# Modulation products: VectorE multiplies and adds up its units, TensorE only sums over the partitions, and its bank joins the ring

## The reference, cut to what matters

```python
mod = jax.nn.silu(c) @ mod_w[l] + mod_b[l]            # 1024 -> 3072
mod_k = jax.nn.silu(c_ctx) @ mod_w[l] + mod_b[l]      # the same matrix, a second vector
shift, scale, gate = jnp.split(mod[:, None, :], 3, axis=-1)
```

## Time and profile before

| | |
|---|---|
| Time, median of 3 runs | 3220.55 us (3218.56 to 3220.67) |
| The profiled execution | 3219.65 us, of which its span is 3217.9 us |
| TensorE busy | 3129.8 us, 97% of the span |
| VectorE busy | 2400.6 us, 75% |
| ScalarE busy | 1240.1 us, 39% |
| Chain that ended last | TensorE 87%, VectorE 8%, ScalarE 4% |
| Mean granted TensorE clock | 0.993 |

### The profile page before, as it was taken

How to read it: one execution, slowest core, us unless ns; L and a number is a source line. 1 busy time by engine, 2 the same in 40 slices (tenths; PEclk the granted TensorE clock), 3 DMA queues, 4 the chain that set the end, 5 groups by cost and what they waited for, 6 DMA issues and landing times.

```text
span 3217.9 us, 37930 instructions
## 1 busy us (share of the span) xinstructions
PE 3129.8 (97%) x14840; PEld 2545.9 (79%) x14840; DVE 2400.6 (75%) x4144; ACT 1240.1 (39%) x1933; POOL 2.2 (0%) x9
## 2 busy tenths in 40 slices
PE   8999999999999999988999999999999999999998
PEld 7878888877988877777878888888777687788887
DVE  6777677768869588878588767667688789789736
ACT  4333233335242455655243223223255533423414
POOL 0000000000000000000000000000000000000000
PEclk9999999999999999999999999999999999999999
DMA  3222212213433450002311111111211222122242
GB/s 128 72 79 79 72 59 73 66 59 125 123 88 126 142 191 8 7 27 90 133 53 46 59 46 53 59 46 53 66 53 52 107 74 70 40 73 93 82 170 73
DMA packets 89249, 250.68 MB, mean 78 GB/s; under 512 B 8560, under 2 KB 24304, under 8 KB 87536
## 3 DMA queue, kind: packets, MB, share of 16 engines
q1 hardware_dynamic: 89072, 248.25, 22.9%
HBM read 204.18 MB, written 44.04 MB: 77 GB/s over the span
## 4 chain that ended last, share of the span: by engine, by line
PE 87%; DVE 8%; ACT 4%; issue 1%; DMA 0%; DVEq 0%; SPq 0%; ACTq 0%
PE PS L543 85%; PE PS L548 2%; DVE WS L2167 1%; DVE X L2175 1%; DVE TMP L2167 1%; DVE X L2167 1%; ACT PT L1294 1%; DVE XS L2175 1%; ACT TMP L1772 1%; DVE COLB L2975 1%; ACT WS L1294 0%; ACT XS L1294 0%; DVE HELD L2224 0%; DVE XSf L2167 0%; DVE PT L2167 0%
## 5 line engine op out<-in xcount | busy, mean ns | idle before, releaser
L543 PE MATMUL PS<-XS,WS 128*128 128x512 f32 (+1 forms) x6480 | 1516.9, 391 | 18.1 <-DVE XS L2167 9.0
L543 PEld LDWEIGHTS PS<-XS,WS 128*128 128x128 f32 x6480 | 1210.3, 188 | 293.5 <-issue 28.8
L543 PE MATMUL PS<-HS,WS 128*128 128x512 f32 x2208 | 515.2, 393 | 13.5 <-DVE HS L2167 10.4
L543 PEld LDWEIGHTS PS<-HS,WS 128*128 128x128 f32 x2208 | 416.9, 189 | 105.3 <-DVE HS L2167 11.2
L1294 ACT ACTIVATE WS<-RAW 128x512 fp32r<-128x512 f32 (+1 forms) x390 | 305.1, 788 | 448.6 <-PE PS L543 393.2
L2167 DVE TENSOR_TENSOR WS<-RAW,WS 128x512 fp32r<-128x512 f32 (+1 forms) x390 | 344.5, 892 | 158.8 <-ACT WS L1294 157.9
L2167 DVE TENSOR_TENSOR X<-PS,X 128x512 f32<-128x512 f32 x272 | 184.4, 689 | 116.1 <-PE PS L543 116.0
L2167 DVE TENSOR_TENSOR TMP<-TMP,PS 128x512 f32<-128x512 f32 x304 | 203.7, 683 | 65.5 <-PE PS L543 59.3
L543 PE MATMUL PS<-T,WS 128*128 128x512 f32 x960 | 230.6, 389 | 0.0
L543 PEld LDWEIGHTS PS<-T,WS 128*128 128x128 f32 x960 | 180.2, 188 | 37.4
L1294 ACT ACTIVATE TMP<-PS 128x512 f32<-128x512 f32 x144 | 85.1, 595 | 306.0 <-PE PS L543 302.3
(11 more groups left out here) (334 smaller groups left out, 3643.4 us busy)
## 6 DMA issues: line engine op xcount, KB each, us to landing
RAW<-in_W SPq DMA_DIRECT2D x258, 512.0 KB, 3.4
RAWX<-in_W SPq DMA_DIRECT2D x35, 512.0 KB, 3.3
DC<-TMP SPq DMA_DIRECT2D x32, 256.0 KB, 2.1
X<-in_xT SPq DMA_DIRECT2D x8, 512.0 KB, 9.4
DX<-X SPq DMA_DIRECT2D x2, 2048.0 KB, 8.5
DCZ<-CA SPq DMA_DIRECT2D x8, 512.0 KB, 4.1
DGA<-TMP SPq DMA_DIRECT2D x16, 256.0 KB, 2.1
DGB<-TMP SPq DMA_DIRECT2D x16, 256.0 KB, 3.2
```

Of the source, the lines that this page charges most:

```text
L543: done = d.matmul(out, l, r, start=first, stop=last)
```

## The change

VectorE now reads a modulation unit raw. For each of its two blocks of 512 columns and each of the two vectors it multiplies by the vector's value of the partition and adds to `HELD`. Nothing is split, no place of `WS` is taken, and TensorE no longer multiplies the units. After four units TensorE sums `HELD` over the partitions by eight matmuls against one column of ones, each with a 128x128 block of `HELD` as fp32 weights. The doubled units lie in blocks 3, 6, 9 and 12 (before: 3, 5, 7 and 9), the turn stands behind m3 of the block that ends a group, and bank 7 is in the ring from the start. The raw slot of a modulation unit comes free when VectorE has worked it, and forms whose raw slot follows such a unit are not written before it is released. The four instructions of `sums` move from the m2 form to the m6 form in both networks.

```diff
-            for _ in range(2 if n in (3, 5, 7, 9) else 1):
+            for _ in range(2 if n in (3, 6, 9, 12) else 1):
                 out.append(("mod", mods))
                 mods += 1
+            turn = ("turn", mods // 4 - 1) if mods // 4 > turned else None
+            turned = mods // 4
         out += [("m1", n + 1) if n < 21 else ("m2", n), ("m4", n), ("m3", n)]
+        if with_mod and turn:
+            out.append(turn)
...
-        f.raws = [ends[earlier[n]] for n in f.loads if n in earlier and forms[ends[earlier[n]]].kind == "raw"]
+        f.raws = [ends[earlier[n]] for n in f.loads if n in earlier and forms[ends[earlier[n]]].kind in ("raw", "vec")]
...
-            sum_at[min(u, pieces[1])] = f.loads
+            sum_at[u] = f.loads
...
-    banks, tmps, misc = Ring(7), Ring(NTMP), Ring(2)
+    banks, tmps, misc = Ring(8), Ring(NTMP), Ring(2)
...
-            e.wait_ge(ac("mod", m), dma("const")("cols"), *banks.free(use))
-            trs([(bank(*use)[:, 4 * j:4 * j + 4], HELD[0:4, m % 2, 128 * j:128 * j + 128], ident[0:4, 0:4])
-                 for j in range(4)]).then_inc(*mm.inc(*use))
...
-            mms([(PS[0:4, 7, :], CVS[:, 2 * q + k, :], blk(us[k], 0, 512)[r], q + k + r == 0, q + k + r == 5)
-                 for k in range(2) for r in range(2)]).then_inc(*mm.inc("mod", n))
...
+            e.wait_ge(ve("mv", 4 * m + 3), ve("ones"), *banks.free(use))
+            for j in range(4):
+                for v in range(2):
+                    done = d.matmul(bank(*use)[:, 2 * j + v:2 * j + v + 1], HELD[:, v, 128 * j:128 * j + 128], ones[:, 0:1],
+                                    start=True, stop=True)
+            done.then_inc(*mm.inc(*use))
...
+        def mod_unit(n):
+            m, q = divmod(n, 4)
+            u = w.take()
+            e.wait_ge(*loaded(u), ac("cv"))
+            for k in range(2):
+                for v in range(2):
+                    x, c = HELD[:, v, :], cvec[:, 2 * q + k, v:v + 1]
+                    if q + k == 0:
+                        d.tensor_scalar(x, raw(u, 512 * k, 512), c, None, ALU.mult).then_inc(*ve.inc("ms", n, k, v))
+                    else:
+                        e.wait_ge(ve("ms", n, 0, v) if k else ve("ms", n - 1, 1, v))
+                        stt(x, raw(u, 512 * k, 512), c, x, ALU.mult, ALU.add).then_inc(*ve.inc("ms", n, k, v))
+            ve.same("mv", n)
+            ve.same("vec", u)
+            release(u)
...
-                if m == 1 and with_mod:
-                    mod_turn(5)
...
-                    e.wait_ge(mm("unit", u) if forms[u].kind == "raw" else w_lo(u))
+                    e.wait_ge(mm("unit", u) if forms[u].kind == "raw" else ve("vec", u) if forms[u].kind == "vec" else w_lo(u))
...
-            for a in (down(columns_of(n)) if what == "down" else [mod[n]]):
+            for a in down(columns_of(n)) if what == "down" else ():
                 k = load(a)
                 forms += [("cols", "turning", (k,), 0), ("cols", "turning", (k,), 1)]
+            if what == "mod":
+                forms.append(("vec", "turning", (load(mod[n]),), 0))
```

More of the change, by code:

```diff
@@ L34, in product_steps @@
 def product_steps(with_mod):
-    out, mods = [], 0
+    out, mods, turned = [], 0, 0
     for n in range(2, 22):
@@ L155, in lay_out @@
         forms.append(f)
-        if kind == "raw":
+        if kind in ("raw", "vec"):
             continue
@@ L228, in next_half @@
             self.halved += 1
-            if f.kind not in ("raw", "hold"):
+            if f.kind not in ("raw", "vec", "hold"):
                 return self.halved - 1
@@ L693, in ffn @@
                 elif what == "mod":
-                    mod_unit(n)
+                    release(w.take())
+                elif what == "turn":
+                    mod_turn(n)
                 else:
@@ L1268, in tensor @@
         ffn("ln1", "x", True)
-        banks.resize(8)
-        banks.ends[7] = ((ac, "mod", 5),)
         latents()
@@ L1396, in turned @@
                     act(hi(k), lo(k), ACT.Copy).then_inc(*ac.inc(name, what, k))
-            def mod_unit(n):
-                m, q = divmod(n, 4)
-                us = [w.take(), w.take()]
-                if q == 3:
-                    e.wait_ge(mm("mod", n))
-                    if m > 1:
-                        e.wait_ge(mm("mt", m - 2))
-                    act(HELD[0:4, m % 2, :], PS[0:4, 7, :], ACT.Copy).then_inc(*ac.inc("mod", m))
-                release(*us)
             us = {fi: (w.take(), w.take()) for fi in (0, 1)}
@@ L1428, in ffn @@
             for what, n in product_steps(with_mod):
+                if what == "turn":
+                    continue
                 if what == "mod":
-                    mod_unit(n)
+                    release(w.take())
                     continue
@@ L2274, in norm @@
                     yield
+        def mod_unit(n):
[13 more added lines that the diff above has]
+            release(u)
         def mod_turn(m):
             e.wait_ge(mm("mt", m), dma("const")("cols"))
-            part = bank("mt", m)[:, 0:16].rearrange("p (a r v) -> p a r v", a=4, r=2)
             out = MOD[:, 4 * m:4 * m + 4, :]
-            tt(out, part[:, :, 0], col("mod_b", 4 * m, 4).unsqueeze(2).to_broadcast([128, 4, 2]), ALU.add).then_inc(*ve.inc("mt0", m))
-            e.wait_ge(ve("mt0", m))
-            tt(out, out, part[:, :, 1], ALU.add).then_inc(*ve.inc("mt", m))
+            tt(out, bank("mt", m)[:, 0:8].rearrange("p (a v) -> p a v", v=2),
+               col("mod_b", 4 * m, 4).unsqueeze(2).to_broadcast([128, 4, 2]), ALU.add).then_inc(*ve.inc("mt", m))
         def ffn(name, tag, with_mod, held):
@@ L2382, in turned @@
                 low(lo, f, hi).then_inc(*ve.inc(name, what, k))
-            def mod_unit(n):
-                m, q = divmod(n, 4)
-                if q == 0 and m:
-                    mod_turn(m - 1)
-                release(w.take(), w.take())
             def down_one(g, m, h):
@@ L3505, in vector @@
         halves()
-        e.wait_ge(ac("cvs"))
-        low(CLO, cvec, CHI).then_inc(*ve.inc("cvs"))
         e.wait_ge(dma("const")("cols"))
@@ L3766, in build @@
             ring.restart()
-        banks.n = 7
+        banks.n = 8
     for s in signals.values():
```

16 lines of the change are left out of this document (1 added, 15 removed).

## The result

The changed kernel takes 3237.48 us (median of 6 runs, 3236.67 to 3238.49), the kernel before 3220.61 us in the same sessions (3218.56 to 3221.26). The ratio is 1.0053, with a 95% interval of 1.0040 to 1.0066: slower by 16.9 us, where 9.9 us of gain were forecast. The profiled execution took 3236.67 us, the least of the six, and spans 3234.8 us (before 3217.9), with a mean granted clock of 0.989 (before 0.993).

The account below looks back on a forecast made before the run. TensorE, busy all of 100 us in the first network, was taken as the bound. Terms -22.3 -2.0 +5.9 +7.0 +4.1 -1.4 -2.5 +1.3 = -9.9 us took 3219.65 to 3209.8, median 3210.7; range 3200 to 3221.

Parts of the forecast that it names:

- the side given 0.09: Outcome that the changed kernel is slower than the one before, above the no-change bound of 3227.0; chance 0.09.
- The double units of blocks 6 and 12: First network, two units behind a down step: VectorE's m6 low part ready before TensorE, no wait, 0 us.
- The double units of blocks 3 and 9: First network: TensorE waits 0.5 at m6 and 3.0 at the next down step, 3.5 us each, +7.0.
- The turns' matmuls: Six new turns, eight fp32 one-column matmuls each: 48 at 0.122 us cost +5.9 (4.0 to 9.2).
- The end of the network: Last down step of the first network: the last unit delays c11, TensorE waits 9.4 instead of 5.33, +4.1 (0 to 7).
- The eighth bank: First down step: the product that waited 2.03 us finds a free bank, the next waits for c11's; -1.4.
- The sums: Second network: moving them off VectorE ahead of the norm starts the norm's chain 2.5 us sooner; -2.5.
- The ring's offset: Attention's first key products find banks not yet emptied and start 3.7 us later, mostly covered; +1.3 (0 to 4).
- The multiplications: First network: TensorE drops four per unit in 24 units, 96 at 0.2325 us, all on the path; -22.3.
- The 12.6 us that followed from the 131 ns: Alternative worth of TensorE's 96 dropped multiplications by the skill's matmul time; forecast would end 9.7 us later, no gain to speak of.
- Rival D: VectorE becomes the bound in every block without a down step, HS waits at all down steps; +25, 3236; chance 0.09.
- Rival C: Loads behind each unit don't overlap, 3.4 us each; blocks 3 and 9 cost 8 each; 3223, no change; chance 0.16.

## Why the prediction was wrong, point by point

The forecast was 3210.7; it came to 3237.5, outside the range and on the side given 0.09.

*The double units of blocks 6 and 12* is the step that failed: "I take 0". The working of blocks 3 and 9 had VectorE 7 us late behind a double, and I asked only whether the next m6 and the next down step would notice. The turn of block 7 was not asked. It stands behind m3, ahead of any down step, and waits for a unit that VectorE reaches behind c22 of that block. Measured: 6.7 us twice, 1.7 us twice more for the turn at half clock, and 2.0 to 2.1 us twice for the product behind it, 21.0 us in all. Two runs show it: without a double in front, or with the turn moved, 16.2 and 14.4 us are gone.

*The double units of blocks 3 and 9* were right: 3.5 us each forecast, with waits of 0.5 and 3.0; measured 0.66 ahead of m6 and 0.62 + 1.67 at the down step, 2.9 us in this execution and 3.3 to 4.1 in five of the other runs, whose block 3 is the same. The mechanism, a load that waits for VectorE's release and lands 3.4 us later, is the right one (3.38 and 3.35 us of idle time behind the units of block 6, where it is plainest). The Trainium skill (DMA: Bandwidth & Descriptors, Anatomy of one DMA) fits a transfer by a fixed 2.0 us and its bytes over 436 GB/s, for transfers that GpSimd issues. For these 512 KB that is an estimate of 3.2 us, with which the trace agrees for a load that is issued alone or first (3.3 to 3.4 us), though SyncE issues them; by the same fit an estimate for loads of half the size is 2.6 us, which no run here shows.

*The turns' matmuls* were mis-sized: 48 at 0.122 us, +5.9, outside bounds of 4.0 to 9.2. The row counts records, and an fp32 matmul leaves two. Measured 0.21 to 0.22 us a matmul, 1.69 a turn, 10.1 for six at full clock. The bound above shared the mistake.

*The end of the network*: 9.4 us of wait forecast, 10.56 measured; the turn stands ahead of it, and TensorE waits so much less. Right within its range, as is its cause: with no unit in the last block the wait is 5.04. The working there adds up to T+11.7 and not T+12.0 for c11, which makes its term 0.3 smaller.

*The eighth bank*: 2.03 became 0.66, the -1.4 of the forecast. *A wait passed over*: the kernel before waits in a third place of this network, 0.68 us for ScalarE's copy of `HELD` ahead of the second turn, and the change takes it away. *The sums*: 2.5 forecast, 2.7 measured. *The ring's offset*: the keys' 3.68 us came as forecast (3.7), and QH's wait fell from 2.35 to 0.29. The clock moved with them: the 12 matmuls of the keys took 4.32 us where they had taken 2.88, the 12 behind QH 3.00 where they had taken 4.57. Later in the attention VectorE is waited for once more, 1.31 us. From the start of the product with ZG (1137.94 us before, 1156.98 with the change) to that of the output product (1521.07 and 1540.83) the changed kernel falls back by 0.7 us, where I had 1.3.

*The multiplications*, -22.3, can be read in the two traces. The down step of block 6 and the product behind it, before and with the change:

```profile
197.26 21.92 PE L543 MATMUL PS<-HS,WS 128*128 128x512 f32 x96
219.95 2.89 PE L543 MATMUL PS<-XS,WS 128*128 128x512 f32 x12
...
194.76 21.92 PE L545 MATMUL PS<-HS,WS 128*128 128x512 f32 x96
216.52 2.88 PE L545 MATMUL PS<-XS,WS 128*128 128x512 f32 x12
```

From start to start these are 22.69 us and 21.76, without a wait in either: 0.93 us for the four multiplications of a unit, 22.3 for 24. The run with the units in the order of the loads agrees: its last down step starts 18.4 us sooner than before (647.20 against 665.56), and -24.3 (with the transposes), +10.2 for turns, -1.4 for the bank and -2.0 for the shorter wait make -17.5. The 12.6 us that followed from the 131 ns of the Trainium skill (TensorE: Matmul & The Clock Gate, Back-to-back issue gap) would have left -7.8, and the run excludes them.

The sum with the measured terms: -24.3, turns +10.1, the waits of blocks 7 and 13 with their clock +21.0, blocks 3 and 9 +5.8, the end +5.2 behind the sixth turn, the wait for ScalarE's copy -0.7, bank -1.4, sums -2.7, attention +0.7: +13.7 of 16.9. Another 1.6 us are the output product of the attention, 192 matmuls that take 45.39 us in the changed kernel's profile and 43.76 before. With the units in the order of the loads they take 43.78 with the same ring, so the ring alone doesn't set it; what does is open. The 1.6 us left are in many small steps and were not traced.

Rival D had the number (3236) and not the mechanism, so that it came near is luck. It wanted waits for HS at all down steps; there were none at 6, 8, 12, 14, 16 and 18, and VectorE with all its load kept TensorE fed in two of the runs. Rival C's sign, loads that land over 5 us behind their slot's release, did show, in the third load behind a unit. But such loads overlap, 3.4, 4.3 and 5.7 us from issue to landing, and don't follow each other by 3.4 us as C had it; blocks 3 and 9 cost 3 to 4 us each and not 8.

## What to carry to other kernels

Work moved to another engine also moves the moment when its input buffer comes free. Ask for each buffer who frees it now, at what place of that engine's order, and what load stands behind it; a unit that is read late holds up loads that other engines read early. The cure was not to place such work where it seems to be cheap but to do it in the order in which the data arrives. And when an engine is reckoned late by some microseconds, follow every later instruction that waits for it, the newly added ones first.

## What the runs showed of the hardware that was not expected

An fp32 matmul with a 128x128 stationary operand and one column leaves two records on TensorE and two weight loads, 0.11 us apart each, 0.21 to 0.22 us for the matmul at full clock and twice that at half. In each 6.7 us wait of a turn the granted clock fell to 0.50, and it was still 0.53 from 256 to 259 us, with work since 251.23; the turn and the product behind it took 3.8 us more for that, so 6.7 us of waiting cost 10.5.

Loads of 512 KB that SyncE issues within a microsecond of each other land one behind the other: 3.4, 4.3 and 5.7 us after their issue behind the second unit of block 6. And VectorE at 74 to 80% beside TensorE cost TensorE nothing: in the run with the units in the order of the loads it was not idle from 100 to 600 us.
